# The low parts of 48 weight tiles are subtracted on VectorE in place of GpSimd

## What is computed

```python
proj = x @ w_in                                   # 1024 -> 2*1024 + 1024 + 1536 + 16 columns
conv_val, conv_gate, z, xbc, dt = jnp.split(proj, [c0, c1, c2, c3], axis=-1)
u = conv_val * jax.nn.sigmoid(conv_gate)
u = causal_depthwise_conv(u, conv_w, conv_b)      # 31 taps
u = jax.nn.silu(layer_norm(u, conv_ln_g, conv_ln_b))
xbc = jax.nn.silu(causal_depthwise_conv(xbc, ssm_conv_w, ssm_conv_b))   # 4 taps
...
y = ssd_chunked(...)                              # 4 chunks of 128 tokens, 16 heads
y = (y + xs_h * d_skip[:, None]).reshape(...) * jax.nn.silu(z)
y = rms_norm(...)                                 # in two groups
return jnp.concatenate([u, y], axis=-1) @ w_out
```

## Time and profile before

| | |
|---|---|
| time, median of 3 runs | 3103.05 us (3100.77 to 3106.71) |
| the profiled execution's own time | 3100.33 us |
| its span on the core | 3098.6 us |
| TensorE busy | 2726.4 us (88%), granted clock 0.927 in the mean |
| VectorE busy | 1570.9 us (51%) |
| ScalarE busy | 1071.9 us (35%) |
| GpSimd busy | 481.7 us (16%) |

### The profile page before, as it was taken

How to read it: one execution, slowest core, us unless ns; L and a number is a source line. 1 busy time by engine, 2 the same in 40 slices (tenths; PEclk the granted TensorE clock), 3 DMA queues, 4 the chain that set the end, 5 groups by cost and what they waited for, 6 DMA issues and landing times.

```text
span 3098.6 us, 29866 instructions
## 1 busy us (share of the span) xinstructions
PE 2726.4 (88%) x11893; PEld 2140.9 (69%) x11893; DVE 1570.9 (51%) x2443; ACT 1071.9 (35%) x1690; POOL 481.7 (16%) x342
## 2 busy tenths in 40 slices
PE   6878696888999989977779989999799899899996
PEld 4656364666888877766667668888568687578885
DVE  3565657535433237956676464332563563543333
ACT  2223343333433222432444343322442353343322
POOL 1021131321000014432311020000101210200001
PEclk7887797999999989989889999999899999899998
DMA  7442211223333322300223123333121142133331
GB/s 205 110 118 68 75 55 29 83 66 91 89 95 95 95 75 82 96 21 21 89 83 96 54 69 96 95 95 96 48 75 55 48 127 64 55 89 95 96 95 54
DMA packets 481274, 251.07 MB, mean 81 GB/s; under 512 B 13534, under 2 KB 478002, under 8 KB 481135
## 3 DMA queue, kind: packets, MB, share of 16 engines
q1 hardware_dynamic: 478516, 242.43, 27.3%
q0 software_dynamic: 1904, 5.73, 0.6%
q10 hardware_dynamic: 715, 1.01, 0.1%
HBM read 247.00 MB, written 2.13 MB: 80 GB/s over the span
## 4 chain that ended last, share of the span: by engine, by line
PE 73%; DVE 16%; ACT 6%; DMA 2%; issue 2%; POOL 1%; SPq 0%; DVEq 0%; ACTq 0%; POOLq 0%
PE ps L741 20%; PE ps L743 20%; PE ps L739 20%; DVE adat L2001 2%; DVE ps L1890 2%; DMA w_f<-in_w_in 2%; PE ps L905 1%; PE ps L1142 1%; PE ps L821 1%; ACT arena_f L1483 1%; DVE hT L2474 1%; ACT wh L1273 1%; DVE w_r L1858 1%; PE ps L890 1%; PE ps L1121 1%
## 5 line engine op out<-in xcount | busy, mean ns | idle before, releaser
L739 PE MATMUL ps<-XH,wh 128*128 128x512 f32 x2160 | 878.8, 407 | 51.0 <-ACT XH L1727 26.5
L743 PE MATMUL ps<-XH,w_r 128*128 128x512 f32 x2160 | 866.3, 401 | 9.9 <-DVE w_r L1858 9.2
L741 PE MATMUL ps<-XL,wh 128*128 128x512 f32 x1968 | 796.2, 405 | 3.9 <-DVE XL L1863 3.9
L1858 DVE TENSOR_TENSOR w_r<-w_f,wh 128x1024 fp32r<-128x1024 f32 x328 | 400.5, 1224 | 556.3 <-ACT wh L1273 556.0
L1273 ACT ACTIVATE wh<-w_f 128x1024 fp32r<-128x1024 f32 (+2 forms) x423 | 429.0, 1017 | 445.3 <-PE ps L743 365.0
L739 PEld LDWEIGHTS ps<-XH,wh 128*128 128x128 f32 x2160 | 418.1, 194 | 172.8 <-ACT XH L1727 30.2
L743 PEld LDWEIGHTS ps<-XH,w_r 128*128 128x128 f32 x2160 | 415.5, 192 | 110.0 <-DVE w_r L1858 12.6
L741 PE MATMUL ps<-arena_r,wh 128*128 128x512 f32 (+1 forms) x1280 | 481.4, 376 | 0.0
L741 PEld LDWEIGHTS ps<-XL,wh 128*128 128x128 f32 x1968 | 380.0, 193 | 96.0 <-DVE XL L1863 7.3
L743 PE MATMUL ps<-arena_r,w_r 128*128 128x512 f32 (+1 forms) x944 | 347.3, 368 | 10.9 <-DVE w_r L1858 8.5
L739 PE MATMUL ps<-arena_r,wh 128*128 128x512 f32 (+1 forms) x944 | 354.5, 375 | 1.4 <-ACT wh L1273 1.4
(11 more groups left out here) (308 smaller groups left out, 2757.4 us busy)
## 6 DMA issues: line engine op xcount, KB each, us to landing
w_f<-in_mlp_w SPq DMA_DIRECT2D x128, 512.0 KB, 3.9
w_f<-in_w_ff SPq DMA_DIRECT2D x64, 512.0 KB, 3.8
w_f<-in_w_in SPq DMA_DIRECT2D x49, 512.0 KB, 3.7
w_f<-in_ada_w SPq DMA_DIRECT2D x48, 512.0 KB, 4.6
w_f<-in_even_w_in SPq DMA_DIRECT2D x36, 512.0 KB, 3.6
w_f<-in_odd_w_in SPq DMA_DIRECT2D x24, 512.0 KB, 3.7
w_f<-in_xa_w_v SPq DMA_DIRECT2D x16, 512.0 KB, 3.5
w_f<-in_even_w_out SPq DMA_DIRECT2D x16, 512.0 KB, 3.6
```

The source lines that it names most:

```text
L739: e.matmul(b, hi[:, k, :], xh, start=u.first and k == 0, stop=False)
L741: e.matmul(b, hi[:, k, :], xl, start=False, stop=False)
L743: last = e.matmul(b, lo[:, k, :], xh, start=False, stop=u.final and k == u.kc - 1)
L1858: e.tensor_tensor(flat(u, 1), flat(u, 0), high_flat(u).bitcast(F32), ALU.subtract).then_inc(dve.sem, dve.up("low", u.n))
```

## The change

The setting of `low` to "pool" in `plan` covers two ranges of units in the kernel before: `cv` up to the first `gate` (first block), and `evg` 0 up to `yout` 7 (the even mixer). The change drops the second range, 48 units: 16 `evg` and `evv`, 12 `xbc`, 8 `z`, 4 `mv`, 8 `yout`. Their `low` is then "dve": `lower_ahead` of GpSimd passes them over, that of VectorE makes them, and TensorE's wait for the low part is on VectorE's semaphore (`low_by[u.low]`, L742). Nothing else differs: loads, high parts, matmuls, slots and the order of all other work are the same.

```diff
     for n, u in enumerate(every):
         u.n, u.raw = n, n % RAW_SLOTS
     by_name = {(u.name, u.m): u for u in every}
-    for u in every[by_name["cv", 0].n:by_name["gate", KC].n] + every[by_name["evg", 0].n:by_name["yout", KC - 1].n + 1]:
+    for u in every[by_name["cv", 0].n:by_name["gate", KC].n]:
         u.low = "pool"
     return plans, every, by_name
```

## The result

The changed kernel takes 3114.73 us in the median (3113.45 to 3116.16, 5 runs), the one before takes 3100.77 us on the same chip (3098.99 to 3106.71, 5 runs). The ratio is 1.0042, 95% interval 1.0027 to 1.0057: slower, by 14.0 us between the medians, where 19.9 was forecast. The profiled execution takes 3116.16 us with a span of 3114.4.

What follows compares the result with a forecast made beforehand. VectorE was taken as full or the bound in three of the four stages touched, level with TensorE in two. 15.8 + 0 - 1.9 + 6.0 = 19.9 us on 3103.05 gave 3123 us, range 3111 to 3135.

Steps and rivals of the forecast that it cites:

- VectorE full, TensorE waiting, in `gv` and `xbc`: `gv` and `xbc`: VectorE becomes the bound, 24 subtractions cost 27.4 us, less idle and blocked time: 15.8 us.
- `y out`: `y out` stage: five more subtractions at 1.14 us, plus 0.3 for TensorE's start at half clock: 6.0 us slower.
- the start of `y out`: `yout` 0 and 1: VectorE makes their low parts sooner than GpSimd, so the pair ends earlier: -2.3 us.
- the +0.4 for late high parts of ScalarE: Gated stage, last two `z` tiles: VectorE's subtractions there delayed by late ScalarE high parts, put at 0.4 us.
- the scan at 0: Scan: six subtractions fall where VectorE waits anyway, 4 us in the mean against 1.14, so cost 0.
- The scan as long as before: Scan: expected sign in the profile after, its length unchanged.
- Faster: Whole kernel: blocked time given back and the quicker start of `y out` outweigh the cost; 3091.5 if all hidden; chance 0.04.
- Slower by 6 to 12: Free time ahead of the subtractions is larger than seen, about half of 15.8 us hidden, 3115 at most; chance 0.12.
- TensorE stays the bound: `gv` and `xbc`: banks take up VectorE's lag, only `y out` costs, 4.1 us, 3107, no change; chance 0.07.
- the scan's subtractions lie on its chain: Scan: late high parts delay `z`, adding 6.8 us, 3134 with blocking; slower by 27 or more, chance 0.12.
- The clock falls in `gv` and `xbc`: `gv` and `xbc`: TensorE's waits bring half clock, up to 103 us over 25 units, from 3150; chance 0.03.
- a sign of being wrong: `gv`: TensorE's clock falling below 1 there was listed among the signs that would show the prediction wrong.

Runs made afterwards that it cites:

- this part alone: Kernel before with only the 30 units `evg` 0 to `z` 1 having their low part made on VectorE: 3120.0 us, ratio 1.0049.
- the half-tap pair: Kernel before and changed kernel, both without the 15 odd taps of the long convolution: 3079.71 us and 3074.81 us.
- the version with five: Kernel before with only the subtractions of `z` 0 and 1 and `yout` 0 to 2 on VectorE: 3095.75 us, ratio 0.9976.
- GpSimd was kept busy: Changed kernel plus four GpSimd 128x256 subtractions for each of the 24 units `evv` 2 to `z` 1: 3120.64 us, ratio 1.0061.

## Why the prediction was right, and where its sizes were off

**Right: VectorE full, TensorE waiting, in `gv` and `xbc`.** 15.8 us were forecast and 16.1 measured (12.6 + 3.5, and 16.0 with this part alone). Every term is seen: steps of 7.00 and 5.82 us, no idle time in front of L1964, L1872 at 0.69 us and L1896 at 0.73, and the half-tap pair shows that the cost hangs on VectorE being full. The two additions took 5.70 us beside GpSimd's subtractions and 1.48 in the version with five. This agrees with the Trainium skill ("SBUF — State Buffer", section "Who interferes with whom"), which says that a VectorE instruction with two SBUF inputs contends with a GpSimd instruction that reads SBUF.

**Right: `y out`,** 6.0 forecast, 5.6 in the changed kernel and 6.1 alone (with 10.0 and 15.2 us of the stage at half clock); TensorE stands 5.1 us once, where about 6 were forecast.

**Right in place, too small in size: the start of `y out`.** The term -2.3 measured -2.7 when only the `yout` units were moved. In the changed kernel the stretch from the scan's end to the first L1941 is 4.2 us shorter, where the terms gave -1.9; the +0.4 for late high parts of ScalarE isn't to be seen (0.1 with the `z` and `mv` units alone). The other 1.5 us do not come from any part alone. TensorE's rate is seen to differ there: of the stretch 24.1 us are at half clock before, 20.7 with the `yout` units alone and 17.2 after. Windows of its first matmuls of `y out`, before and after:

```profile
1512.00:1518.00 6.00, 3.92 (x8) 0.50 0.00 0
1518.00:1524.00 6.00, 6.00 (x20) 0.68 0.00 0
```

```profile
1528.00:1534.00 6.00, 5.50 (x20) 0.76 0.00 0
```

Before, TensorE is at half clock until 1521.8 us, 6.1 us after its first matmul with a low part (1515.73); after, until 1530.9, 2.3 us after it (1528.57).

**The step that failed in size: the scan at 0.** Right is that the six subtractions cost nothing there, and take nothing away (143.5 with them and without). What the sum left out is that the scan can get shorter without an edit in it: it lost 2.5 us, with 25.0 us of it at half clock in place of 34.3. "The scan as long as before" was wrong. That this step cost no more is luck: the same scan took 4.9 us more than after when GpSimd was kept busy ahead of it. With -2.5 here, -2.3 at the start, -0.7 in `norm`, +0.3 in `gv` and `xbc` and -0.4 in `y out` the forecast 19.9 becomes 14.3. The rest of the distance between 3123 and 3114.73 is mostly the base: the sum was set on 3103.05, and the kernel before took 3100.77 beside it.

**The rivals.** "Faster" fell: the gain in blocked time is real, but only where the subtraction is moved alone. "Slower by 6 to 12", which had about half of the 15.8 us hidden, fell with the 16.1 measured, and "TensorE stays the bound" with the steps above; "the scan's subtractions lie on its chain" with the run that moved those alone. "The clock falls in `gv` and `xbc`" came once in `gv`, for 3.4 us, which the prediction named as a sign of being wrong. TensorE in that place, after:

```profile
1234.00:1237.30 3.30, 1.19 (x4) 1.00 0.55 159
1237.40:1240.70 3.30, 3.30 (x9) 0.50 0.00 0
1240.80:1244.00 3.20, 3.20 (x15) 1.00 0.00 0
```

It cost nothing that can be seen: VectorE's steps there have no idle time behind 1236 us, and by 1244.4 TensorE waits for VectorE again. Over the windows the granted clock was 0.96 and 0.94, against 0.98 and 0.95.

**Open.** That the scan's length and TensorE's time at half clock go together holds in every profile, those with all taps and the half-tap pair each among themselves. It is not shown by an experiment that sets the clock alone. Neither a longer wait ahead of the scan nor the engine of its subtractions places the stretches; what does isn't known, and nothing was run that moved the scan's start alone by known small steps. The 1.5 us of the start go with 3.5 us less at half clock there, but no run separates them. The 0.7 us of `norm` can't be put down to it in this way: the stage has more half clock after (10.5 us) than before (8.6).

## What to carry to other kernels

Before moving work to an engine, take its busy time in the very stretch and not over the span: at 51% in the mean VectorE had 2.4 us free in 145, and each moved subtraction cost what it lasts there, while the same move cost nothing once VectorE had less to do. Collisions of the two engines are worth removing one by one: five moved subtractions gave -7.1 us, of which 4.7 (2.0 in `xbc`, 2.7 at the start) can be put down to them, and all 48 gave +14.0. Look first at what the held instruction will meet once the one beside it is gone, as with `evg` 7.

## What the runs showed of the hardware

- Stage lengths measured inside one profile are the same to 0.1 us in the two profiles of the kernel before, from `gv` to `norm`, while the timed runs of that kernel scatter by 3 us or more. `gv` took 77.0 us in all seven profiles of kernels that had nothing edited ahead of its end. One profile of each kernel so told apart what eleven timed runs did not; but a stage that wasn't edited can still change, as the scan did.
- Where TensorE is at half clock is not chance either. A scan whose matmuls are the same took 141.0 us (two kernels), 143.1 to 143.3 (five), 143.5 (three, one of them twice) or 146.0, with 25.0, 33, 34.3 and 40.1 us of it at half clock.
- Holding goes both ways. A VectorE addition of 0.69 us takes up to 2.75 beside a GpSimd subtraction of 2.4; and four short GpSimd instructions take 4.06 us in place of 3.07 beside a VectorE subtraction. The 96 short ones (0.77 us each) cost only 2.0 us in 160.
